# Head norm of queries and keys in two parts, a copy moved up on ScalarE, and two gate-bias loads moved to the front of the DMA queue

## The reference

```
for l in range(2):
    hn   = rms_norm(x, ln1);  proj = hn @ w_in
    mq, mk = rope(rms_norm(heads(mq))), rope(rms_norm(heads(mk)))   # 6 + 6 heads of 64: first run
    y_moba = causal attention(mq, mk, mv)
    qk     = silu(causal_depthwise_conv(xqk));  i_pre = xi + igate_b;  f_pre = xf + fgate_b
    y_ml   = rms_norm(mlstm(qk, xv, i_pre, f_pre) * sigmoid(xo))
    sq, sk = rope(rms_norm(heads(sq))), rope(rms_norm(heads(sk)))   # 6 + 2 heads: second run
    y_swa  = windowed attention with sinks(sq, sk, sv)
    x = x + concat(y_moba, y_ml, y_swa) @ w_out
    x = x + relu(rms_norm(x, ln2) @ w_up)^2 @ w_down
```

## Time and profile before

| | before |
|---|---|
| median of three runs | 1818.25 us |
| the profiled execution | 1819.21 us |
| its span | 1817.4 us |
| PE busy | 1770.4 us (97%) |
| DVE busy | 1148.2 us (63%) |
| ACT busy | 950.2 us (52%) |
| POOL busy | 44.3 us (2%) |
| chain that ended last | PE 90%, DVE 4%, ACT 2%, POOL 1% |

### The profile page before, as it was taken

How to read it: one execution, slowest core, us unless ns; L and a number is a source line. 1 busy time by engine, 2 the same in 40 slices (tenths; PEclk the granted TensorE clock), 3 DMA queues, 4 the chain that set the end, 5 groups by cost and what they waited for, 6 DMA issues and landing times.

```text
span 1817.4 us, 23998 instructions
## 1 busy us (share of the span) xinstructions
PE 1770.4 (97%) x9920; PEld 1461.1 (80%) x9920; DVE 1148.2 (63%) x1351; ACT 950.2 (52%) x1286; POOL 44.3 (2%) x32
## 2 busy tenths in 40 slices
PE   7899999998999999999999999999999999999998
PEld 6768888786888889777888897688888787778887
DVE  5876555586755665477656755677556655776555
ACT  5554455545545554465445644656455546654443
POOL 0100000010000000000000000000000000000000
PEclk9999999999999999999999999999999999999999
DMA  8565555755555565755655556537555656355651
GB/s 271 162 209 162 185 187 190 248 164 179 193 188 196 193 222 197 233 180 167 224 193 185 186 176 205 192 114 240 186 186 186 231 166 228 101 178 171 195 191 70
DMA packets 226003, 342.07 MB, mean 188 GB/s; under 512 B 7684, under 2 KB 116584, under 8 KB 225896
## 3 DMA queue, kind: packets, MB, share of 16 engines
q1 hardware_dynamic: 225080, 339.27, 56.8%
q10 hardware_dynamic: 816, 1.28, 0.2%
HBM read 339.48 MB, written 1.05 MB: 187 GB/s over the span
## 4 chain that ended last, share of the span: by engine, by line
PE 90%; DVE 4%; ACT 2%; issue 1%; POOL 1%; DMA 1%; SPq 1%; DVEq 0%; POOLq 0%; ACTq 0%
PE PS L1876 15%; PE PS L1878 15%; PE PS L1877 15%; PE PS L1930 14%; PE PS L1931 7%; PE PS L1918 2%; PE PS L1919 2%; PE PS L1920 2%; PE PS L2257 1%; PE PS L1962 1%; PE PS L2315 1%; PE PS L2259 1%; PE PS L2258 1%; PE PS L2338 1%; PE PS L2326 1%
## 5 line engine op out<-in xcount | busy, mean ns | idle before, releaser
L1168 DVE TENSOR_TENSOR LO<-RAW,HI 128x2048 fp32r<-128x2048 f32 (+1 forms) x272 | 619.6, 2289 | 293.3 <-ACT HI L652 292.3
L652 ACT CAST HI<-RAW 128x2048 fp32r<-128x2048 f32 (+1 forms) x272 | 517.7, 1909 | 162.9 <-PE PS L1878 131.8
L1930 PE MATMUL PS<-AHL,HI 128*128 128x512 f32 x1120 | 396.4, 399 | 0.0
L1931 PE MATMUL PS<-AHL,LO 128*128 128x256 f32 x1120 | 314.4, 281 | 0.0
L1876 PE MATMUL PS<-HI,AHL 128*128 128x512 f32 (+2 forms) x672 | 247.3, 368 | 8.7 <-ACT Z L652 7.2
L1930 PEld LDWEIGHTS PS<-AHL,HI 128*128 128x128 f32 x1120 | 210.4, 188 | 52.0
L1876 PE MATMUL PS<-HI,HIDH 128*128 128x512 f32 x640 | 250.1, 391 | 0.0
L1877 PE MATMUL PS<-LO,HIDH 128*128 128x512 f32 x640 | 249.2, 389 | 0.0
L1878 PE MATMUL PS<-HI,HIDL 128*128 128x512 f32 x640 | 249.1, 389 | 0.0
L1877 PE MATMUL PS<-LO,AHL 128*128 128x512 f32 (+2 forms) x672 | 241.7, 360 | 0.0
L1878 PE MATMUL PS<-HI,AHL 128*128 128x512 f32 (+2 forms) x672 | 241.5, 359 | 0.0
(11 more groups left out here) (286 smaller groups left out, 2218.7 us busy)
## 6 DMA issues: line engine op xcount, KB each, us to landing
RAW<-in_w_ff SPq DMA_DIRECT2D x96, 1024.0 KB, 5.3
RAW<-in_w_in SPq DMA_DIRECT2D x78, 1024.0 KB, 5.2
RAW<-in_w_mod SPq DMA_DIRECT2D x48, 1024.0 KB, 5.1
RAW<-in_w_up SPq DMA_DIRECT2D x32, 1024.0 KB, 5.4
RAW<-in_w_down SPq DMA_DIRECT2D x32, 1024.0 KB, 5.0
RAW<-in_w_o SPq DMA_DIRECT2D x12, 1024.0 KB, 5.0
RAW<-in_w_out SPq DMA_DIRECT2D x8, 1024.0 KB, 7.0
RAW<-in_w_attn_out SPq DMA_DIRECT2D x6, 1024.0 KB, 5.1
```

The lines of the kernel that those rows point to most:

```text
L652: return nc.scalar.copy(dst, src)
L1168: tt(LO[:, c % RAW_N, 0:n], RAW[:, c % RAW_N, 0:n], HI[:, NTH[c] % HL_N, 0:n].bitcast(F32), ALU.subtract).then_inc(s_lo, 1)
L1930: mm(PS[:, b + q, :], wh, AHL[:, j, :, :].rearrange("p a n -> p (a n)"), start=j == 0, stop=False)
L1931: ins = mm(PS[:, b + q, 0:256], wl, AH[:, j, :], start=False, stop=j == KT - 1)
```

## The change

1. The two gate-bias loads (IFB) get a semaphore of their own and are issued right behind x, ahead of the six constants and chunk 0; the number of parameter rows falls from 11 to 9. DVE waits for the two before `gates()`, and for the rows (with the two small tables) only behind `gate_sums()` and the split of chunk 3.
2. The squares, the power and the first product of the first run are done in two parts: heads 0 to 7 as soon as the copy of c0+4 is made (16 numbers on POOL), heads 8 to 11 behind c0+5 (8 numbers).
3. On DVE `qk_norm(0)` moves ahead of the product with the sigmoid, and the split of c0+9 moves behind `qk_cos(0)`.
4. On ACT the copy of c0+9 moves ahead of `exps(1)`.

```
@@ sync
+            sp.dma_start(IFB[:, :, 0:4], a["igate_b"].partition_broadcast(P)).then_inc(s_ifb, 16)
+            sp.dma_start(IFB[:, :, 4:8], a["fgate_b"].partition_broadcast(P)).then_inc(s_ifb, 16)
             const(PR0[64:72, :], ...)
...
-                rows(IFB[:, :, 0:4], a["igate_b"])
-                rows(IFB[:, :, 4:8], a["fgate_b"])
@@ gpsimd
-                for j, width in enumerate((2, 24, 2 * (NQK - 12), 8, 2)):
-                    rsqrt(5 * l + j, width)
+                rsqrt(5 * l, 2)
+                pool.wait_ge(s_msa, l + 1)
+                nc.gpsimd.tensor_tensor(RS[:, 32:48], MS[:, 32:48], NHALF[:, 0:16], ALU.pow).then_inc(s_rsa, 1)
+                for j, width in enumerate((8, 2 * (NQK - 12), 8, 2)):
+                    rsqrt(5 * l + 1 + j, width)
@@ scalar
                     if k == 4:
                         copy_group(1, c0 + k, Z[:, :, 0:512], 512)
+                        act.wait_ge(s_gfree, g0 + 4)
+                        nc.scalar.activation(QK[:, :, 0:8, :]..., Z[:, :, 0:512], ACT.Square).then_inc(s_sqa, 1)
                     if k == 5:
                         copy_group(0, c0 + k, Z[:, :, 512:768], 256)
                         act.wait_ge(s_gfree, g0 + 5)
-                        nc.scalar.activation(QK[:, :, 0:12, :]..., Z[:, :, 0:768], ACT.Square).then_inc(s_sq, 1)
+                        nc.scalar.activation(QK[:, :, 8:12, :]..., Z[:, :, 512:768], ACT.Square).then_inc(s_sq, 1)
...
                 weights_turned(0)
+                copy_group(0, c0 + 9, Z[:, :, 1280:1792], 512)
                 exps(1)
                 weights_turned(1)
-                copy_group(0, c0 + 9, Z[:, :, 1280:1792], 512)
@@ vector
-            dve.wait_ge(s_row, 16 * N_ROWS)
-            (NSK, C32: three small instructions)
...
+                def first_squares():
+                    dve.wait_ge(s_sqa, l + 1)
+                    link(nc.vector.tensor_reduce(MS[:, 32:48]..., QK[:, :, 0:8, :], AX_X, ALU.add))
+                    ts(MS[:, 32:48], MS[:, 32:48], 1.0 / DH, EPS, ALU.mult, ALU.add).then_inc(s_msa, 1)
...
                 def qk_norm(r):
+                    if r == 0:
+                        dve.wait_ge(s_rsa, l + 1)
+                        tt(q[:, :, 0:8, :], z[:, :, 0:8, :], rs (16 numbers), ALU.mult)
+                        (the rest of the function's first product on heads 8 to 11)
...
+                if not l:
+                    dve.wait_ge(s_ifb, 32)
                 gates()
...
                 gate_sums()
                 if not l:
                     ahead(c0)
+                    dve.wait_ge(s_row, 16 * N_ROWS)
+                    (NSK, C32: the three small instructions)
...
                 ahead(c0 + 4)
+                first_squares()
                 convolve(1, 2)
                 qk_squares(0)
                 ahead(c0 + 5)
+                qk_norm(0)
                 dve.wait_ge(s_sg, l + 1)
                 tt(CV[:, :, :], CV[:, :, :], SG[:, :, :], ALU.mult).then_inc(s_lqk, 1)
-                ahead(c0 + 6)
-                qk_norm(0)
                 qk_sin(0)
                 qk_cos(0)
+                ahead(c0 + 6)
```

More of the change, by code:

```diff
@@ L342, in build @@
         s_xin = sem("x_loaded")
+        s_ifb = sem("gate_biases_loaded")
         s_raw = [sem(f"raw_loaded_{i}") for i in range(RAW_N)]
@@ L362, in build @@
         s_rs = sem("rstd_done")
+        s_sqa = sem("first_heads_squares")
+        s_msa = sem("first_heads_mean_squares")
+        s_rsa = sem("first_heads_rstd")
         s_src = sem("transpose_source")
@@ L832, in _ @@
                         copy_group(1, c0 + k, Z[:, :, 0:512], 512)
+                        act.wait_ge(s_gfree, g0 + 4)
+                        nc.scalar.activation(QK[:, :, 0:8, :].rearrange("p t h d -> p t (h d)"),
+                                             Z[:, :, 0:512], ACT.Square).then_inc(s_sqa, 1)
                     if k == 5:
@@ L835, in _ @@
                         act.wait_ge(s_gfree, g0 + 5)
-                        nc.scalar.activation(QK[:, :, 0:12, :].rearrange("p t h d -> p t (h d)"),
-                                             Z[:, :, 0:768], ACT.Square).then_inc(s_sq, 1)
+                        nc.scalar.activation(QK[:, :, 8:12, :].rearrange("p t h d -> p t (h d)"),
+                                             Z[:, :, 512:768], ACT.Square).then_inc(s_sq, 1)
                     if k == 6:
@@ L1339, in parts @@
                     return QK[:, :, h1:h2, :], z.rearrange("p t (h d) -> p t h d", d=DH), h2 - h1, gains
+                def first_squares():
+                    dve.wait_ge(s_sqa, l + 1)
+                    link(nc.vector.tensor_reduce(MS[:, 32:48].rearrange("p (t h) -> p t h", t=NT), QK[:, :, 0:8, :], AX_X,
+                                                 ALU.add))
+                    ts(MS[:, 32:48], MS[:, 32:48], 1.0 / DH, EPS, ALU.mult, ALU.add).then_inc(s_msa, 1)
                 def qk_squares(r):
                     q, z, n, _ = parts(r)
+                    if r == 0:
+                        q, n = QK[:, :, 8:12, :], 4
                     dve.wait_ge(s_sq, 2 * l + r + 1)
@@ L1348, in qk_norm @@
                     q, z, n, gains = parts(r)
+                    if r == 0:
+                        dve.wait_ge(s_rsa, l + 1)
+                        rs = RS[:, 32:48].rearrange("p (t h) -> p t h", t=NT).unsqueeze(3)
+                        tt(q[:, :, 0:8, :], z[:, :, 0:8, :], rs.to_broadcast((P, NT, 8, DH)), ALU.mult)
+                        q2, z2, n2 = q[:, :, 8:12, :], z[:, :, 8:12, :], 4
+                    else:
+                        q2, z2, n2 = q, z, n
                     dve.wait_ge(s_rs, 5 * l + 2 + r)
-                    rs = RS[:, 0:2 * n].rearrange("p (t h) -> p t h", t=NT).unsqueeze(3)
-                    link(tt(q, z, rs.to_broadcast((P, NT, n, DH)), ALU.mult))
+                    rs = RS[:, 0:2 * n2].rearrange("p (t h) -> p t h", t=NT).unsqueeze(3)
+                    link(tt(q2, z2, rs.to_broadcast((P, NT, n2, DH)), ALU.mult))
                     for i, (h1, h2) in enumerate(gains):
@@ L1424, in _ @@
                     ahead(c0)
+                    dve.wait_ge(s_row, 16 * N_ROWS)
+                    link(ts(NSK[:, :, :], SK[:, :, :], -1.0, None, ALU.mult))
+                    dve.wait_ge(s_cs, 1)
+                    link(nc.vector.memset(C32[:, :, :], 0.0))
+                    tt(C32[:, :, 0:2].rearrange("p k s -> p s k"), PAR[:, 64:80].rearrange("p (s k) -> p s k", s=2),
+                       SGC[:, :].rearrange("p (s k) -> p s k", s=2), ALU.mult).then_inc(s_c4, 1)
                 ahead(c0 + 1)
@@ L2465, in _ @@
                 mlp(q.mlp, q.c_mlp, q.u + 3, q.m_mlp, None, tiles=q.tile(1, 1, 0))
-N_CONST, N_ROWS = 11, 11
+N_CONST, N_ROWS = 11, 9
 INPUTS = ["x", "ln1", "w_in", "conv_w", "conv_b", "igate_b", "fgate_b", "mlstm_norm", "moba_q_norm", "moba_k_norm",
```

## The result

Four runs of the changed kernel lie between 1805.29 and 1805.92 us, median 1805.44. Four runs of the kernel before give 1818.86 (1817.3 to 1820.38). The ratio is 0.9927, 95% interval 0.991 to 0.9944: 13.4 us, or 0.7%, faster. The forecast was 1802.7 with a range of 1800.0 to 1809.5, so the range holds and the forecast itself is 2.7 us too low; the measured time is within 0.3 us of the 1805.2 of rival A. The profiled execution took 1805.92 us over a span of 1803.8: 13.3 us less where 15.6 was forecast.

The account below looks back on a forecast made before the run. PE, busy 97% of the span, was taken as the bound. Gates 2.1 us and two layers 13.5 us together save 15.6 us, giving 1802.7 us against the median 1818.25; range 1800 to 1809.5.

Parts of the forecast that it names:

- rival A: Start: the two IFB loads cost their upper bound, 3.7 us, making the gates -0.4 us; total 1805.2 us; chance 15%.
- The copy: ACT copy of c0+9 moved ahead of exps(1): PE's 3.61 us stall and 1.5 us low clock go, 5.1 us per layer.
- Rival C: Transposes needing exps(1): PE's wait for c0+10 returns there, costing 2.6 us per layer; 1807.8 us; chance 11%.
- The norm: Two-part norm on DVE and POOL: rotated heads ready before PE's transposes, so PE's 1.63 us wait goes in each layer.
- rival B: Split of c0+9 on DVE ends late and PE waits there: up to 3.3 us come back; 1806.0 us; chance 9%.
- The gates: Layer 0, line 2038: PE's 1.6 us wait and 1.7 us low clock go, 3.3 us, less 1.2 us at the start.
- The front of the queue: Two IFB loads ahead of constants and chunk 0 delay the start: 1.2 us taken, near issue time, between 0 and 3.7.
- A's sign: At the start: ACT's first cast at 13 or later would show the front of the queue costing its upper bound.
- the ring: Two repeated-row loads ahead of chunk 0 hold the queue 1.0 us each, 2.0 us, counted only in the upper bound.
- the clock's rise: At the start: it may slip by one low stretch, 1.7 us, counted only in the upper bound of 3.7 us.
- Rival D: Whole kernel: loads, casts and splits set the pace, PE waits for LO or HI instead; slower, 1823 us; chance 2%.

Follow-up runs that it names:

- the gate part alone: Kernel before with only the gate biases loaded in front and DVE's row wait moved behind gate_sums: 1818.14 us, 0.9994.
- the norm in one part: Changed kernel with the norm undivided (one square of 12 heads, one power of 24 numbers), DVE's new order kept: 1812.68 us, 0.9968.
- the old order: Changed kernel with the two-part norm, but product with the sigmoid and a split ahead of the norm on DVE, as before: 1804.2 us, 0.9921.
- the doubled front: Changed kernel with two more gate-bias loads on 128 partitions behind the first two, 1024 pieces ahead of the constants: 1806.91 us, 0.9937.
- the norm alone: Kernel before with only the norm in two parts and DVE's new order: 1815.69 us, 0.998.
- the copy alone: Kernel before with only the ACT copy of c0+9 moved ahead of exps(1): 1806.37 us, 0.9932.

## Why the prediction was right, and where it was not

**The copy: right.** ACT's timeline after, to set beside the earlier trace rows (all times after stand 0.28 us earlier than in the frame of before, by the exponent product):

```profile
83.56 1.07 ACT L659 COPY Z<-PS 128x512 f32<-128x512 f32 x2
85.88 0.40 ACT L873 ACTIVATE PM<-PM,NB 128x128 f32<-128x128 f32 x1 [1.25 <-DVE NB L1506]
88.12 1.06 ACT L901 ACTIVATE QK<-Z 128x1024 f32<-128x1024 f32 x1
```

The copy lies in ACT's idle stretch, and 1.25 us of it are left, so `exps(1)` is not delayed. The clock behind is full, with 50 products in 5.50 us where 14 took 3.06:

```profile
89.50:95.00 5.50, 5.50 (x50) 5.17 (x47) 4.87 (x16) 2.66 (x11) 2.90 (x1) 1.00 0.00 0
```

Rival C, a stall at the exps, comes to no more than the one added wait of 0.3 us at line 2117.

**The norm: right, in each step.** POOL and DVE after:

```profile
55.73 3.08 POOL L640 TENSOR_TENSOR RS<-MS,NHALF 128x16 f32<-128x16 f32 x1 [46.55 <-DVE MS L1349]
59.82 3.61 POOL L634 TENSOR_TENSOR RS<-MS,NHALF 128x8 f32<-128x8 f32 x1 [1.01 <-DVE MS L1357]
```

```profile
55.56 3.38 DVE L1398 SCALAR_TENSOR_TENSOR CV<-XP,PAR,CV 128x256 f32<-128x256 f32 x8
...
59.65 2.28 DVE L1178 TENSOR_TENSOR LO<-RAW,HI 128x2048 fp32r<-128x2048 f32 x1
61.85 1.22 DVE L1364 TENSOR_TENSOR QK<-Z,RS 128x1024 f32<-128x1024 f32 x1
63.46 0.69 DVE L1370 TENSOR_TENSOR QK<-Z,RS 128x512 f32<-128x512 f32 x1 [0.39 <-POOL RS L634]
...
71.71 0.95 DVE L1391 TENSOR_TENSOR QK<-QK,Z 128x768 f32<-128x768 f32 x1
72.58 2.28 DVE L1178 TENSOR_TENSOR LO<-RAW,HI 128x2048 fp32r<-128x2048 f32 x1
```

The power of 8, just ahead of a split, takes 3.61 us (3.7 taken), and DVE waits 0.39 us for it (0.3 forecast). The heads end at 72.66 (72.9 forecast), PE transposes at 75.10 without a wait, and the split of c0+9 ends at 74.86 (75.2): rival B did not come. The power of 16 ran beside the convolution, whose instructions read two inputs from SBUF, and took 3.08 us where it takes 2.90 alone; had it been held through the whole convolution, it would have ended near 61.9 and not at 58.81. The Trainium skill (GPSIMD Engine Reference, Specifications) says that POOL is in contention with DVE instructions that have two SBUF inputs. The trace agrees for the split, with 2 us on the power of 8, and hardly for eight short instructions in a row, with 0.2 us on the power of 16.

**The gates: the stall went as forecast.** The wait of 1.61 us is gone, and so is the low clock behind it in this profile (57 products in 6.40 us, against 18 in 3.40 in the earlier trace rows):

```profile
32.20:38.60 6.40, 6.40 (x57) 6.40 (x55) 5.44 (x9) 4.61 (x6) 0.00 (x0) 1.00 1.07 371
```

From the gate products to the exponent product it takes 6.43 us instead of 8.02, 1.59 less. Together 3.2 us (3.3 forecast). The second half of that is not sure to be there: the two kernels with a wait of 1.2 us at the gates had no low clock behind it.

**The front of the queue: the mis-sized term.** I took 1.2 us between bounds of 0 and 3.7, and by the issue time, "since that is the one part that surely is there". It measured 2.9 us. Two things make it up, and both are rival A's, which had 15%. So the right mechanism was named, but only as a rival, and another was taken for the sum. That the time lies in the range is partly luck: the forecast's own range ended at 1805, and the room above it was made for A, B and C together. A's sign, a first cast at 13 or later, did not come (12.61). First, the ring. The first cast went from 10.68 to 12.61:

```profile
12.61 1.95 ACT L659 CAST HI<-RAW 128x2112 fp32r<-128x2112 f32 x1 [1.15 <-DMA RAW<-in_w_in]
```

and PE's first product on chunk 0 from 15.96 to 17.89, 1.93 us. The experiments say what it is: two loads with 2 pieces each cost 0.1 us or less, and twice the pieces cost a little over twice (4.2 us). What counts is how long the pieces ahead take, not when SP issued the load. The Trainium skill (DMA: Bandwidth & Descriptors, Queues, rings and completion order) says that on each DMA engine descriptors are consumed in ring order. The trace agrees: chunk 0 lands behind the biases, and later by what they take. The near price was in the earlier trace rows all the time, 1.0 us per load of repeated rows; I had it as the upper bound and should have taken it. My reason against it, that x still fills the engines, was wrong from 6 us on: there the DMA share is 0.20 and 0.40.

Second, the clock's rise. The start before, in two windows, and after:

```profile
15.96:19.28 3.32, 3.32 (x15) 3.32 (x16) 3.32 (x7) 3.30 (x3) 0.00 (x0) 1.00 0.84 288
19.28:23.20 3.92, 3.92 (x34) 3.92 (x34) 3.28 (x2) 1.39 (x2) 0.00 (x0) 1.00 0.34 89
```

```profile
17.89:23.78 5.89, 5.89 (x27) 5.89 (x28) 5.89 (x8) 4.69 (x4) 0.00 (x0) 1.00 0.65 218
23.78:26.60 2.82, 2.82 (x25) 2.82 (x25) 0.71 (x1) 0.00 (x0) 0.00 (x0) 1.00 0.30 81
```

Count the products. 15 in 3.32 us and 27 in 5.89 us are 0.22 us each; 34 in 3.92 and 25 in 2.82 are 0.115 and 0.113. The first are at 1.2 GHz, the second at 2.4, though the column of the granted clock reads 1.00 in all four. After the change 12 more products run at the slow spacing, and the stretch from chunk 0 to the gate products, without its wait, grew from 13.28 to 14.28 us: 1.0 us. That this belongs to the two loads is not shown. Of the kernels with them in front four have 13.2 (the gate part alone, the norm in one part, the old order, the doubled front), and only changed has more, 14.3 and 14.4 in its two profiles; of the eight without them five have 13.2 to 13.7 (the kernel before and the norm alone among them) and three 11.7 to 11.9. Changed repeats its own value, so the 1.0 us may well be that kernel's; what in it sets the clock's rise is not known. So 1.93 us of the 2.9 is shown to be the change's, and the last 1.0 us stays open.

The sum of the start: 3.2 - 2.9 = 0.3 us gained, where 2.1 was forecast. That is 1.8 of the 2.3 us missed in the profiled execution. The layers gave 0.4 us more than the 13.5 forecast, and 0.3 us lie outside the span. The other 0.6 us were lost in the first pass behind the layers, where the prediction had said that nothing should be given back. They go with the change on DVE: that pass takes 113.15 to 113.27 us in the kernel before, the copy alone and the gate part alone, and 113.63 to 114.26 in the norm alone, in changed and in every other kernel that touches DVE's norm, its order included. PE's wait of 0.4 us for DVE's MOD is there in changed and in the norm alone (0.9 us in the old order) and missing in the three others. How a change nearly 300 us earlier on DVE brings it about is not shown.

**Rival D**, that the chunks are the pace, was wrong for the mixer: no wait for a chunk appeared but the 0.3 us for LO that was there before. For the first 40 us, though, it is true. Every kernel that freed the start found the next landing late, and all ended at 1803.5 to 1804.0. The simplest of these is the change without its gate part, 1803.79 us; the lowest, with chunk 3 ahead of the rows, 1803.49. Both lie under the changed kernel on the medians, by 0.1%, with intervals that overlap.

## What to carry to other kernels

With PE near 98% busy, look for copies and small steps that stand behind something still being computed, while their own input has long been ready: one such line moved into an idle stretch of its engine was worth 5.2 us per layer, of which 1.5 was clock. Price a load that is moved to the front of a queue by the time its pieces hold the ring, from the landings of its like, and not by its issue; and when one load is moved forward, ask at once which landing is late next. An operation split in two pays when it lets the longer part run before the last input comes; the order around it mattered less than the split.

## What the runs showed of the hardware

- Two loads that repeat rows of 16 bytes on 128 partitions (512 pieces) delayed the first cast on the 1 MB load behind them by 1.55 to 2.05 us against the kernel before (five profiles: 12.23 to 12.73, against 10.61 to 10.83 in eight without them); four such loads delayed it by 4.2 us (14.88). While they were moved the DMA share fell to 0.20 and the rate to 19 GB/s. Two loads of one partition delayed it by 0.1 us or less, though the issue slipped 1.2 us.
- A POOL power of 8 numbers took 3.61 us where a 2.28 us split began just as it started, and 1.64 us alone. A power of 16 beside eight short convolution instructions took 3.08 us, 2.90 alone. The profile's spans on POOL are rough, but DVE's own wait confirms the 3.61: it ended at 63.46, with the power's end at 59.82 + 3.61 = 63.43.
- The same wait of 3.6 us was followed by 3.06 us of products at 1.2 GHz in one profile and by 5.65 us in another; waits of 1.6 and 2.5 us at the gates by 3.4 us, a wait of 1.2 us by none (twice).
- Before a trace's first change of the clock, its column reads 1.00 even where products are 0.22 us apart. The spacing of the products is the safer reading.
